# Mixture-of-experts tiles cut in four quarters of 32 rows instead of two halves of 64, with three quarters' weights copied, in a two-block transformer kernel

## The chip, the cores and the metric

One core of one Trainium2 chip runs the whole program. The metric is the device time of one execution in microseconds (us), lower is better. Three runs of the kernel before gave 2169.46, 2170.88 and 2175.67 us, so the median is 2170.88 us.

## The reference, cut to what matters

The program is a transformer block followed by two further blocks (`l` = 0 and 1). Each of these two ends in a mixture of experts over 768 tokens (block 0: 512 of the sequence and 256 of the context) or 512 tokens (block 1). A token has 1024 values; there are 16 experts in 4 groups; each token takes one group and in it two experts.

```python
a = jnp.einsum('nd,edf->nef', h, w_gate[g])      # 1024 -> 256, per expert
u = jnp.einsum('nd,edf->nef', h, w_up[g])        # 1024 -> 256
hid = jax.nn.silu(a) * u * combine[:, g, :, None]
out = out + jnp.einsum('nef,efd->nd', hid, w_down[g])   # 256 -> 1024
```

So block 0 has 1536 (token, expert) rows and block 1 has 1024. An expert's weights in float32 are 2 MB for gate and up together and 1 MB for down, 48 MB over the 16 experts of a block. Worked out from the reference and its inputs, the rows per expert are 72 to 132 in block 0 and 35 to 89 in block 1.

## The kernel before, in words

`Router` and `Dispatch` work out which expert each token takes and sort the rows into **tiles of 128 rows**. A tile has two **halves** of 64 rows, each half of one expert; `pairs_bound` gives 20 tiles in block 0 and 16 in block 1, whatever the routing. `mo.pace` spreads the experts over the tiles, and `k.last_pair[e]` holds the last tile that needs expert e.

`Experts` then runs over the tiles t. `tensor` (PE) does, per tile: gate/up, 8 chunks of 128 in the contraction, each chunk one matmul for the low half (L2356, moving operand straight from the expert's place) and one for the high half (L2357, moving operand from a copy `mo.wgu`); then down of tile t-1 (L2337, L2338, the high half from the copy `mo.wd`); then the transposes of `hid` (L2368) and of the gathered rows of tile t+2 (L2322). The two halves write partitions 0 to 63 and 64 to 127 of one PSUM bank. `gpsimd` (POOL) gathers a tile's 128 rows from DRAM by an indirect DMA (L2516), `mo.xg` has two buffers, so the gather of tile t waits for the transposes of tile t-2. ACT (ScalarE) and DVE (VectorE) copy the high half's weights (L2412, L2478 for gate/up; L2418, L2484 for down), bring transposes out of PSUM, and ACT stores the finished tile (L2402). All of these buffers are double.

The weights come through `ExpertLoads.fill` on the SP queue, in an order that is written out. There are three **places** of 3 MB; expert e goes to place e % 3:

```python
sp.wait_ge(self.gu_full[0], last + (self.gu_full[1] + 1))     # L2241
for j in range(2):
    sp.dma_start(k.places[:, a, j, :], self.w[e, j])...       # L2242, gate/up, 2 x 1 MB
if e:
    self.announce_down(sp, e - 1)                             # waits until down of e-1 landed
sp.wait_ge(k.gu_landed[a].sem, ...)                           # L2246
...
sp.dma_start(k.places[:, a, 2, :], self.w[e, 2])...           # L2249, down, 1 MB
```

Before an expert's gate/up goes out, SP waits until the last tile that used the place has done its gate/up; before its down, until that tile has done its down (`y_full`). An announcement lets the copying engines use what landed. While an expert's down is under way, the gate/up of the next may be issued.

After the last tile every stage meets (L3290), and `CombineProject` (block 0) or `Combine` (block 1) gathers each token's two result rows (L2618, L2539) and adds them to the residual rows `k.X`, six tiles of 1024 columns.

Of the kernel before, what the change touches and what calls it, by code (L numbers as in the profile page):

```python
# [17 lines left out]
F32 = mybir.dt.float32  # L18
# [33 lines left out]
PLACES = 3  # L52
HALF = 64
# [12 lines left out]
def shape_constants():  # L66
# [40 lines left out]
    halves = [2 * pairs_bound(n * P) for n in (NT, ST)]  # L107
    c["pace"] = np.tile(np.array([[(x + 1) * h // NEXP for x in range(NEXP)] for h in halves], np.float32), (P, 1, 1))
# [1853 lines left out]
class Router(Stage):  # L1962
# [4 lines left out]
    def __init__(self, k, l, tiles, rows):  # L1967
        super().__init__(k)
        self.l, self.tiles, self.rows_out = l, tiles, rows
# [6 lines left out]
        self.consts = k.small_landed.reserve(64 + 16 * (1 + (len(tiles) > ST)))  # L1976
        self.freed = k.places_free.reserve(1)

    def gpsimd(self, pool, ch):
        k = self.k  # L1980
        loads = [(k.mo.iota, k.C["iota"]), (k.mo.token, k.C["token"]), (k.mo.before, k.C["before"]),
                 (k.mo.pace, k.C["pace"][:, self.l, :])]
        loads += k.gate_loads(self.l, 5, 1 + (len(self.tiles) > ST))
        for dst, src in loads:
            pool.dma_start(dst, src).then_inc(k.small_landed.sem, 16)
        pool.wait_ge(k.small_landed.sem, self.consts + 16 * len(loads))
# [48 lines left out]
    def await_consts(self, eng):  # L2035
        eng.wait_ge(self.k.small_landed.sem, self.consts + 64 + 16 * (1 + (len(self.tiles) > ST)))
# [70 lines left out]
def pairs_bound(tokens):  # L2107

    return ((2 * tokens - NEXP) // HALF + NEXP + 1) // 2


class Dispatch(Stage):


    def __init__(self, k, n, router):
        super().__init__(k)
        self.n, self.m, self.router = n, pairs_bound(n * P), router
# [4 lines left out]
    def tensor(self, pe):  # L2122
# [8 lines left out]
        for u in range(2 * n):  # L2131
            last = pe.matmul(self.banks.bank(2)[:, 0:2 * self.m], mo.row_hot[:, u, :], mo.pair_hot[:, u, 0:2 * self.m],
# [3 lines left out]
    def vector(self, dve, ch):  # L2136
# [16 lines left out]
        at, at_pair, at_row = (x[:, 0:2 * n] for x in (mo.at, mo.at_pair, mo.at_row))  # L2153
# [14 lines left out]

        do(dve.tensor_scalar(mo.count, mo.count, 1.0 / HALF, None, ALU.mult))
        count_of(mo.halves, mo.count, NEXP, 2 * n - 1, ALU.is_gt)  # L2170
        do(dve.tensor_scalar(mo.halves, mo.halves, 1.0, None, ALU.add))
        do(dve.tensor_tensor_scan(mo.end, mo.ones[:, 0:NEXP], mo.halves, 0.0, ALU.mult, ALU.add))

        do(dve.tensor_scalar(mo.spare, mo.end[:, NEXP - 1:NEXP], -1.0, float(2 * m), ALU.mult, ALU.add))
# [4 lines left out]
        do(dve.tensor_tensor(mo.first, mo.end, mo.halves, ALU.subtract))  # L2179
        do(dve.scalar_tensor_tensor(rank, over_tokens(mo.first), float(HALF), rank, ALU.mult, ALU.add))  # L2180
        for i in range(2):
# [4 lines left out]
        count_of(at_pair, at_row, 2 * n, m - 1, ALU.is_ge)  # L2186
        do(dve.scalar_tensor_tensor(at_row, at_pair, -float(P), at, ALU.mult, ALU.add))
        pairs = mo.pair_hot[:, 0:2 * n, 0:m]
        ch.step(dve.tensor_tensor(pairs, mo.iota[:, 0:m].unsqueeze(1).to_broadcast((P, 2 * n, m)),
                                  at_pair.unsqueeze(2).to_broadcast((P, 2 * n, m)), ALU.is_equal))  # L2190
# [3 lines left out]
        for i in range(2):  # L2194
            half = pairs[:, n * i:n * i + n, :]
            dve.tensor_tensor(mo.pair_hot[:, n * i:n * i + n, m:2 * m], half,
# [4 lines left out]
        ended = mo.ended[:, 0:2 * m * NEXP].rearrange("p (h e) -> p h e", e=NEXP)  # L2201
        do(dve.tensor_tensor(ended, mo.iota[:, 0:2 * m].unsqueeze(2).to_broadcast((P, 2 * m, NEXP)),
                             mo.end.unsqueeze(1).to_broadcast((P, 2 * m, NEXP)), ALU.is_ge))
        do(dve.tensor_reduce(mo.expert[:, 0:2 * m], ended, AXX, ALU.add))
        do(dve.tensor_scalar(mo.expert[:, 0:2 * m], mo.expert[:, 0:2 * m], float(NEXP - 1), None, ALU.min))
        dve.tensor_copy(k.half_expert[:, 0:2 * m], mo.expert[:, 0:2 * m])
        do(dve.tensor_scalar(mo.last, mo.end, 0.5, -0.5, ALU.mult, ALU.add))
        count_of(mo.count, mo.last, NEXP, m - 1, ALU.is_ge)
        dve.tensor_copy(k.last_pair[:, :], mo.count)
# [6 lines left out]
class ExpertLoads:  # L2216


    def __init__(self, k, l, A, router, dispatch, gu_full, y_full):
        self.k, self.w, self.gu_full, self.y_full = k, A["experts"][l], gu_full, y_full  # L2220
        self.n0 = k.rg.lend(self)
        self.freed, self.lists = router.freed, dispatch.ready
# [3 lines left out]
        self.ready = k.experts_ready.reserve(2 * NEXP)  # L2226
        self.early = []

    def fill(self, sp):
        k = self.k  # L2230
        sp.wait_ge(k.weights_used, self.n0)
        for e in range(NEXP):
            a = e % PLACES
            if e == PLACES - 1:
                sp.wait_ge(k.places_free.sem, self.freed + 1)
            if e == PLACES:
                sp.wait_ge(k.lists_ready.sem, self.lists + 1)
            if e >= PLACES:
                last = sp.value_load(k.last_pair[0:1, e - PLACES:e - PLACES + 1], min_val=0, max_val=63)
                sp.wait_ge(self.gu_full[0], last + (self.gu_full[1] + 1))  # L2240
            for j in range(2):  # L2241
                sp.dma_start(k.places[:, a, j, :], self.w[e, j]).then_inc(k.gu_landed[a].sem, 16)  # L2242
            if e:
                self.announce_down(sp, e - 1)
# [10 lines left out]
        for n in self.early:  # L2255
            k.rg.load(sp, n)
# [1145 lines left out]
```

## Time and profile before

| | |
|---|---|
| runs, median (lowest to highest) | 2170.88 us (2169.46 to 2175.67) |
| the profiled execution, its own time | 2169.99 us |
| its span, first to last instruction | 2168.2 us |
| granted TensorE clock, mean | 0.976 of full |
| PE, DVE, ACT, POOL busy | 94%, 46%, 28%, 9% of the span |
| DMA | 311.64 MB, mean 144 GB/s |
| Experts stage of block 0, first gate/up to last down | 1374.6 to 1612.5 us |
| Experts stage of block 1, the same | 1949.0 to 2141.6 us |

Shares over the span are means of stages that are bound by different things; the two Experts stages are a fifth of the time. Times in the rows are microseconds from the start of the span, durations in microseconds unless ns stands there.

### The profile page before, as it was taken

The page shows a single profiled execution, that of the slowest core. Times are in us where ns is not written, and L with a number is a line of the kernel's source. Part 1 is how long each engine was busy: PE and PEld are TensorE (multiplying, and loading weights), DVE is VectorE, ACT ScalarE, POOL GpSimd, SP SyncE. Part 2 cuts the span into 40 slices and gives each one's busy share as a digit, 9 for nine tenths or more (in the row PEclk, how much of TensorE's full clock was granted, in tenths as well). Part 3 has the DMA queues.
Part 4 walks back from the last instruction along what each step waited for, and adds up shares of the span by engine and source line. Part 5 has one row for each costly group of instructions (what it writes and reads, how often), then busy time and mean ns, then how long its engine had stood idle before and what let it go on. Part 6 is the DMA issues. An engine that isn't in the chain of part 4 may idle for free.

```text
span 2168.2 us, 26578 instructions
## 1 busy us (share of the span) xinstructions
PE 2033.5 (94%) x10088; PEld 1107.5 (51%) x10088; DVE 989.7 (46%) x1778; ACT 616.2 (28%) x1302; POOL 188.7 (9%) x222
## 2 busy tenths in 40 slices
PE   7999999999999999898998998999989999989994
PEld 4555874444444444456456745533335688463331
DVE  2002771487777001378736524423218577253333
ACT  2002660100000001422225503334325566033331
POOL 3000110011111000022100000101001000011101
PEclk9999999999999999999999999999999999989997
DMA  8433101576765321211201004678853200067885
GB/s 266 133 78 127 40 11 39 193 242 227 244 241 211 117 68 60 84 39 40 73 6 60 18 3 168 248 296 309 299 183 135 76 3 2 1 253 286 336 327 207
DMA packets 103868, 311.64 MB, mean 144 GB/s; under 512 B 8839, under 2 KB 42791, under 8 KB 85312
## 3 DMA queue, kind: packets, MB, share of 16 engines
q1 hardware_dynamic: 73360, 178.50, 23.5%
q0 software_dynamic: 22576, 103.09, 13.7%
q10 hardware_dynamic: 7808, 28.35, 3.3%
q8 instruction: 84, 1.38, 0.3%
q14 instruction: 40, 0.33, 0.0%
HBM read 280.47 MB, written 34.68 MB: 145 GB/s over the span
## 4 chain that ended last, share of the span: by engine, by line
PE 76%; issue 7%; DVE 5%; DMA 5%; PEld 3%; ACT 2%; SPq 0%; POOL 0%; PEldq 0%; POOLq 0%; DVEq 0%; ACTq 0%
PE ps L2857 14%; PE ps L312 8%; PE ps L337 8%; PE ps L2356 7%; PE ps L1623 6%; PE ps L806 5%; DMA wide<-in_experts 4%; PE ps L852 4%; PE ps L827 4%; PE ps L2660 4%; PE ps L2337 3%; PE ps L1599 2%; PEld ps L1379 2%; PE ps L1028 1%; PE ps L1379 1%
## 5 line engine op out<-in xcount | busy, mean ns | idle before, releaser
L2857 PE MATMUL ps<-wide 128*128 128x512 f32 x704 | 306.0, 594 | 2.3 <-issue 1.3
L2356 PE MATMUL ps<-wide,Z 128*64 x576 | 254.9, 595 | 2.1 <-DVE Z L2459 2.1
L2357 PE MATMUL ps<-T,Z 128*64 128x512 f32 x576 | 254.9, 596 | 0.0
L2857 PEld LDWEIGHTS ps<-wide 128*128 128x128 f32 x704 | 132.6, 190 | 171.7 <-issue 170.4
L2356 PEld LDWEIGHTS ps<-wide,Z 128*64 128x64 f32 x576 | 75.9, 137 | 152.0 <-issue 152.0
L1623 PE MATMUL ps<-wide 128*128 128x512 f32 (+1 forms) x384 | 148.3, 543 | 0.5 <-issue 0.5
L2337 PE MATMUL ps<-wide,Z 128*64 x288 | 131.2, 599 | 4.9 <-ACT Z L2418 4.9
L1150 DVE SCALAR_TENSOR_TENSOR Z<-Z,wide 128x2048 f32<-128x2048 f32 x56 | 131.6, 2350 | 2.8
L2338 PE MATMUL ps<-Z 128*64 128x512 f32 x288 | 131.3, 599 | 0.0
L806 PE MATMUL ps<-T 64*128 64x256 f32 (+1 forms) x888 | 109.7, 377 | 7.8 <-DVE nm L940 5.9
L1379 PE MATMUL ps<-wide 128*128 128x512 f32 x256 | 114.6, 607 | 1.8 <-issue 1.1
L373 ACT ACTIVATE T<-ps 128x512 f32<-128x512 f32 (+2 forms) x139 | 70.6, 536 | 133.5 <-PE ps L1379 111.1
L1623 PEld LDWEIGHTS ps<-wide 128*128 128x128 f32 x384 | 71.8, 190 | 68.6 <-issue 65.3
L872 ACT ACTIVATE T<-T,nm 128x768 f32<-128x768 f32 (+3 forms) x112 | 86.7, 775 | 68.0 <-DVE nm L940 68.0
L312 PE MATMUL ps<-wide 128*128 128x512 f32 x224 | 98.6, 602 | 6.7 <-POOLq L3290 3.9
L806 PEld LDWEIGHTS ps<-T 64*128 64x128 f32 x888 | 86.1, 191 | 29.2 <-issue 14.0
L3176 DVE TENSOR_TENSOR X<-ps,X 128x512 f32<-128x512 f32 x16 | 11.1, 692 | 196.6 <-PE ps L312 103.7
L852 PE MATMUL ps<-T,Z 128*64 128x128 f32 x1504 | 98.9, 278 | 0.4 <-ACT wide L888 0.4
L337 PE MATMUL ps<-wide 128*128 128x512 f32 x224 | 97.1, 594 | 0.3
L375 DVE COPY T<-ps 128x512 f32<-128x512 f32 (+2 forms) x113 | 69.7, 637 | 59.8 <-PE ps L1379 49.8
L2873 ACT ACTIVATE Z<-ps 128x512 f32<-128x512 f32 x22 | 13.1, 597 | 293.2 <-PE ps L2857 293.1
L2412 ACT ACTIVATE T<-wide 128x2048 f32 x36 | 68.6, 1906 | 78.5 <-SPq L2246 52.6
(383 smaller groups left out, 3029.5 us busy)
## 6 DMA issues: line engine op xcount, KB each, us to landing
wide<-in_experts SPq DMA_DIRECT2D x96, 1024.0 KB, 7.9
Z<-in_mod_w POOLq DMA_DIRECT2D x32, 1024.0 KB, 5.2
moe_out<-Z ACTq DMA_DIRECT2D x36, 512.0 KB, 5.8
X<-in_mod_w POOLq DMA_DIRECT2D x16, 1024.0 KB, 5.3
wide<-in_w_gate SPq DMA_DIRECT2D x22, 512.0 KB, 5.3
wide<-in_w_up SPq DMA_DIRECT2D x22, 512.0 KB, 6.8
wide<-in_w_in SPq DMA_DIRECT2D x10, 1024.0 KB, 9.1
wide<-in_w_down SPq DMA_DIRECT2D x10, 1024.0 KB, 5.2
```

The costliest lines, as they stand in the source:

```text
L312: last = pe.matmul(self.banks.bank(u0 + i)[0:self.rows, 0:cn], self.lhs(k0 + c, t), w[:, c, :], start=(k0 + c == 0), stop=(k0 + c == self. ...
L337: last = pe.matmul(self.banks.bank(u0 + i)[:, 0:cn], self.lhs(k0 + c, t), w[:, c, :], start=(k0 + c == 0), stop=(k0 + c == self.nk - 1))
L806: last = pe.matmul(self.S(i, h)[:, at:at + m], q, keys, start=True, stop=True)
L852: last = pe.matmul(k.ps[64 * h:64 * h + 64, 7, t * P:(t + 1) * P], u["values"][b](h), self.PT[:, j % 2, h, b * P:(b + 1) * P], start=(b * ...
L1150: ins = dve.scalar_tensor_tensor(acc, w, by, acc, ALU.mult, ALU.add)
L1379: last = pe.matmul(self.banks.bank(u), w, k.HT[:, c, 0:SEQ], start=(c == 0), stop=(c == DK - 1))
L1623: last = pe.matmul(self.lin.bank(u)[:, 0:cn], k.HT[:, c, t * P:(t + 1) * P], w[:, c % 4, :], start=(c == 0), stop=(c == DK - 1))
L2337: pe.matmul(ps[low, 5 + hf, :], mo.hidT[:, p, c, low], w.columns(e, 2, at), start=(c == 0), stop=(c == 1))
L2338: last = pe.matmul(ps[high, 5 + hf, :], mo.hidT[:, p, c, high], mo.wd[:, p, at:at + 512], start=(c == 0), stop=(c == 1))
L2356: pe.matmul(ps[low, p, :], mo.xT[:, p, c, low], w.columns(e, j, at), start=(c == 0), stop=(c == DK - 1))
L2357: last = pe.matmul(ps[high, p, :], mo.xT[:, p, c, high], mo.wgu[:, p, j, at:at + 512], start=(c == 0), stop=(c == DK - 1))
L2857: last = pe.matmul(self.gu.bank(u)[:, 0:self.n], w, self.rhs(c), start=(c == 0), stop=(c == DK - 1))
```

## The change

A tile of 128 rows now has four **quarters** of 32 rows (`QUARTER = 32`), each of one expert. `quads_bound` gives 16 tiles in block 0 and 12 in block 1. Worked out from the routing, in block 0 tile t is expert t in all four quarters, except that one quarter of tile 13 is expert 12; in block 1 the tiles are 0 0 0 1, 1 1 2 2, 2 3 3 3, 4 4 4 5, 5 5 6 6, 6 7 7 7, 8 8 8 9, 9 9 10 10, 10 11 11 11, 12 12 12 13, 13 13 14 14, 14 15 15 15. Each quarter's matmul writes 32 partitions. Quarter 0 reads the place, quarters 1, 2, 3 read copies: DVE copies for quarters 1 and 2, ACT for quarter 3. There is one buffer where there were two for the copies, `xg`, `xT`, `ysb`, `silu`, `hid`; the gate/up copies are made in two parts (chunks 0 to 3 after `gu_half`, chunks 4 to 7 after `gu_full`).

There are four gate/up places (in `wide`) and four down places (in `T`). The down of expert e is loaded after the gate/up of expert e + `LAG`. To make room, residual tiles 3 to 5 (block 0) or 2 and 3 (block 1) are written to DRAM by POOL in the Router stage and read back by SP after the last tile is stored; `ysb`, `xT`, `xg` and the row gate of block 1 lie in `k.X`. The gates of block 0 are loaded at the end by SP instead of by POOL in the Router.

```diff
-PLACES = 3
-HALF = 64
+PLACES = 4
+QUARTER = 32
+LAG = 3
-def pairs_bound(tokens):
-    return ((2 * tokens - NEXP) // HALF + NEXP + 1) // 2
+def quads_bound(tokens):
+    return ((2 * tokens - NEXP) // QUARTER + NEXP + 3) // 4
@@ Router.gpsimd
-        loads += k.gate_loads(self.l, 5, 1 + (len(self.tiles) > ST))
-        for dst, src in loads:
+        for dst, src in loads + [self.spill]:
             pool.dma_start(dst, src).then_inc(k.small_landed.sem, 16)
@@ ExpertLoads.fill
-        for e in range(NEXP):
-            a = e % PLACES
+        for e in range(PLACES):
             if e == PLACES - 1:
                 sp.wait_ge(k.places_free.sem, self.freed + 1)
...
+            self.load_gate_up(sp, e)
+        self.router.await_rows(sp)
+        for e in range(PLACES):
+            self.load_down(sp, e)
+        for e in range(PLACES):
+            self.announce_gate_up(sp, e)
+        for e in range(PLACES):
+            self.announce_down(sp, e)
+        sp.wait_ge(k.lists_ready.sem, self.lists + 1)
+        for e in range(PLACES, NEXP + LAG):
+            if e - PLACES >= PLACES:
+                self.announce_down(sp, e - PLACES)
+            if e < NEXP:
+                sp.wait_ge(self.gu_full[0], self.last_of(sp, e - PLACES) + (self.gu_full[1] + 1))
+                self.load_gate_up(sp, e)
+                self.announce_gate_up(sp, e)
+            d = e - LAG
+            if d >= PLACES:
+                sp.wait_ge(self.y_full[0], self.last_of(sp, d - PLACES) + (self.y_full[1] + 1))
+                self.load_down(sp, d)
         self.announce_down(sp, NEXP - 1)
...
+        sp.wait_ge(self.y_full[0], self.y_full[1] + self.m)
+        for dst, src in self.gates:
+            sp.dma_start(dst, src).then_inc(k.gates_landed.sem, 16)
+        sp.wait_ge(self.y_stored[0], self.y_stored[1] + 16 * self.m)
+        for dst, src in self.back:
+            sp.dma_start(dst, src).then_inc(k.tiles_back.sem, 16)
+    def announce_gate_up(self, sp, e):
+        k, a = self.k, e % PLACES
+        sp.wait_ge(k.gu_landed[a].sem, self.gu_landed[a] + 32 * (e // PLACES + 1))
+        sp.drain().then_inc(k.gu_ready.sem, 1)
@@ Experts.tensor
+        def gate_up(t, e, j):
+            for c in range(4 * j, 4 * j + 4):
+                at = 512 * (c % 4)
+                for q, rows in enumerate(quarters):
+                    w_rows = mo.wgu[:, q - 1, j, at:at + 512] if q else w.gate_up(e, j, at, 512)
+                    last = pe.matmul(ps[rows, t % 2, :], mo.xT[:, c, rows], w_rows, start=(c == 0), stop=(c == DK - 1))
+            return last
@@ Experts.vector, the new order
+        first_rows(0)
+        x_out(0)
+        last_rows(0)
+        for t in range(m):
+            if t + 1 < m:
+                first_rows(t + 1)
+                x_out(t + 1)
             self.after(dve, self.silu_ready, t + 1)
...
+            if t + 1 < m:
+                last_rows(t + 1)
+            if t:
+                y_out(t - 1)
             down_copy(t)
+        y_out(m - 1)
@@ Experts.gpsimd
         for t in range(self.m):
-            gather(t)
+            if t:
+                self.after(pool, self.x_transposed, t)
```

The SP queue in the steady part of block 0, before (L2242 is an expert's gate/up, L2249 its down, the TENSOR_LOAD reads the last tile that used the place):

```order
L2242 DMA wide<-in_experts 128x2048 [waits moe_gu_full]
L2242 DMA wide<-in_experts 128x2048
L2249 DMA wide<-in_experts 128x2048 [waits down_landed_0,gate_up_landed_1,moe_y_full]
L2239 TENSOR_LOAD last_pair
L2239 ISA x2
L2240 REGISTER_ALU
L2242 DMA wide<-in_experts 128x2048 [waits moe_gu_full]
L2242 DMA wide<-in_experts 128x2048
L2249 DMA wide<-in_experts 128x2048 [waits down_landed_1,gate_up_landed_2,moe_y_full]
```

And in the changed kernel, from the down of expert 4 on (L2280 is gate/up, L2284 down):

```order
L2284 DMA T<-in_experts 128x2048 [waits moe_y_full]
L2275 TENSOR_LOAD last_quad [waits down_landed_0]
L2275 ISA x2
L2253 REGISTER_ALU
L2280 DMA wide<-in_experts 128x2048 [waits moe_gu_full]
L2280 DMA wide<-in_experts 128x2048
L2275 TENSOR_LOAD last_quad [waits gate_up_landed_0]
L2275 ISA x2
L2258 REGISTER_ALU
L2284 DMA T<-in_experts 128x2048 [waits moe_y_full]
```

The wait for an expert's down to land stood behind the next gate/up's issue; now it stands ahead of it, and a second TENSOR_LOAD stands between gate/up and down.

The POOL queue, block 0, before (gathers of the tiles' rows):

```order
L2516 DMA Z<-moe_rows,row_token 128x1024 [waits small_landed,rows_stored,stage_done]
L2516 DMA Z<-moe_rows,row_token 128x1024
L2516 DMA Z<-moe_rows,row_token 128x1024 [waits moe_x_transposed] x18
```

And changed:

```order
L2554 DMA X<-moe_rows,row_token 128x1024 [waits small_landed,rows_stored,stage_done]
L2554 DMA X<-moe_rows,row_token 128x1024 [waits moe_x_transposed] x15
```

The second gather went out at once; now each but the first waits for the transposes of the tile just before it.

## Rows read from the trace of the kernel before

**Rows 1.** The page, part 1: engine, busy us, share of the span, instructions.

```profile
PE 2033.5 (94%) x10088; PEld 1107.5 (51%) x10088; DVE 989.7 (46%) x1778; ACT 616.2 (28%) x1302; POOL 188.7 (9%) x222
```

**Rows 2.** Timeline, PE, one tile of block 0: start, us, engine, line, operation, tiles, count.

```profile
1441.78 0.44 PE L2368 MATMUL ps<-ident,Z 128*128 128x128 f32 x2
1442.05 1.04 PE L2322 MATMUL ps<-ident,Z 128*128 128x128 f32 x8
1443.02 0.64 PE L2356 MATMUL ps<-wide,Z 128*64 x1
1443.02 0.64 PE L2357 MATMUL ps<-T,Z 128*64 128x512 f32 x1
...
1454.71 0.64 PE L2356 MATMUL ps<-wide,Z 128*64 x1
```

**Rows 3.** Groups by line, whole span: count, then busy us and mean ns.

```profile
L2356 PE MATMUL ps<-wide,Z 128*64 x576 | 254.9, 595 | 2.1 <-DVE Z L2459 2.1
L2478 DVE COPY T<-wide 128x2048 f32 x36 | 44.4, 1233 | 62.0 <-SPq L2246 58.4 <-issue 3.5
L2412 ACT ACTIVATE T<-wide 128x2048 f32 x36 | 68.6, 1906 | 78.5 <-SPq L2246 52.6 <-issue 13.9 <-DVEq L3290 12.0
L2484 DVE COPY Z<-wide 128x1024 f32 x36 | 24.6, 684 | 0.0
```

**Rows 4.** Timeline, PE: first gate/up of block 0, then of block 1, last down.

```profile
1374.60 0.64 PE L2356 MATMUL ps<-wide,Z 128*64 x1 [1.05 <-DVE Z L2459]
...
1611.94 0.59 PE L2337 MATMUL ps<-wide,Z 128*64 x1
...
1949.02 0.64 PE L2356 MATMUL ps<-wide,Z 128*64 x1 [1.04 <-DVE Z L2459]
...
2141.04 0.59 PE L2337 MATMUL ps<-wide,Z 128*64 x1
```

**Rows 5.** Chain of waits, block 1: start, us, what; the first and another of eight.

```profile
1970.88 11.56 DMA wide<-in_experts
1983.90 11.31 DMA wide<-in_experts
```

**Rows 6.** Stages of both blocks: busy us of the engines, then PEclk, DMA share, GB/s.

```profile
1374.00:1613.00 239.00, 235.33 (x1152) 88.19 (x1152) 71.24 (x99) 93.96 (x120) 20.52 (x18) 0.99 0.72 266
1949.00:2142.00 193.00, 187.18 (x920) 70.12 (x920) 64.38 (x78) 66.06 (x79) 15.25 (x14) 1.00 0.78 292
```

**Rows 7.** Timeline, SP queue, block 1: issues of gate/up (x2) and down (x1).

```profile
1903.41 0.81 SPq L2242 DMA_DIRECT2D wide<-in_experts  x2
1910.85 0.33 SPq L2249 DMA_DIRECT2D wide<-in_experts  x1
...
1982.54 0.33 SPq L2249 DMA_DIRECT2D wide<-in_experts  x1
1983.52 1.62 SPq L2242 DMA_DIRECT2D wide<-in_experts  x2
...
1996.55 0.89 SPq L2242 DMA_DIRECT2D wide<-in_experts  x2
```

**Rows 8.** Expert weights, the down issued at 1910.85, Router stage of block 1.

```profile
DMA to landing us min/median/max: 4.8/4.8/4.8
```

**Rows 9.** Expert weights, the gate/up issued at 1520.32, block 0.

```profile
DMA to landing us min/median/max: 5.5/7.2/8.8
```

**Rows 10.** Expert weights, the down issued at 1515.28, block 0.

```profile
DMA to landing us min/median/max: 6.4/6.4/6.4
```

**Rows 11.** Gathers of tile rows, block 0, 1380 to 1610.

```profile
DMA to landing us min/median/max: 5.0/7.8/11.5
```

**Rows 12.** Timeline, PE, mod stage: four column quarters, 16 passes of 512 columns.

```profile
465.53 1.92 PE L1127 MATMUL ps<-Z,wide 128*32 128x512 f32 x16
```

**Rows 13.** Timeline, PE: passes after a pause, end of block 0 and of block 1.

```profile
1607.27 1.11 PE L2337 MATMUL ps<-wide,Z 128*64 x1 [2.19 <-ACT Z L2418]
...
1608.17 1.06 PE L2337 MATMUL ps<-wide,Z 128*64 x1
...
1610.65 0.59 PE L2337 MATMUL ps<-wide,Z 128*64 x1
...
2137.99 0.64 PE L2337 MATMUL ps<-wide,Z 128*64 x1 [2.67 <-ACT Z L2418]
...
2138.47 0.59 PE L2337 MATMUL ps<-wide,Z 128*64 x1
```

**Rows 14.** Timeline, start of block 0: the second tile's gate/up (PE).

```profile
1384.54 0.64 PE L2356 MATMUL ps<-wide,Z 128*64 x1
```

More of the change, by code:

```diff
@@ L2304, in after @@
         eng.wait_ge(s[0], s[1] + tiles)
-    def run(self, eng, prologue, step, epilogue):
-        prologue()
-        for t in range(self.m):
-            step(t // 2, t % 2, t == self.m - 1)
-        epilogue(self.m // 2, self.m % 2)
     def tensor(self, pe):
@@ L2335, in down @@
                 for c in range(2):
-                    at = 1024 * c + 512 * hf
-                    pe.matmul(ps[low, 5 + hf, :], mo.hidT[:, p, c, low], w.columns(e, 2, at), start=(c == 0), stop=(c == 1))
-                    last = pe.matmul(ps[high, 5 + hf, :], mo.hidT[:, p, c, high], mo.wd[:, p, at:at + 512],
-                                     start=(c == 0), stop=(c == 1))
+                    for q, rows in enumerate(quarters):
+                        at = 512 * hf
+                        w_rows = mo.wd[q - 1][c][:, at:at + 512] if q else w.down(e, 1024 * c + at, 512)
+                        last = pe.matmul(ps[rows, 5 + hf, :], mo.hidT[:, c, rows], w_rows, start=(c == 0), stop=(c == 1))
             last.then_inc(self.y_full[0], 1)
-        keep_awake(pe, k, 7, 17 if m > 16 else 30)
+        keep_awake(pe, k, 7, 17 if m > ST * 3 else 30)
         x_transposes(0)
-        e = w.expert_of(pe, 0)
-        before = None
+        e, before = w.expert_of(pe, 0), None
         for t in range(m):
-            p = t % 2
-            self.after(pe, self.gu_act, t + 1)
-            self.after(pe, self.gu_dve, t + 1)
+            self.after(pe, self.first_act, t + 1)
+            self.after(pe, self.first_dve, t + 1)
             self.after(pe, self.x_out_act, t + 1)
@@ L2353, in tensor @@
                 self.after(pe, self.hid_ready, t - 1)
-            for c in range(DK):
-                j, at = c // 4, 512 * (c % 4)
-                pe.matmul(ps[low, p, :], mo.xT[:, p, c, low], w.columns(e, j, at), start=(c == 0), stop=(c == DK - 1))
-                last = pe.matmul(ps[high, p, :], mo.xT[:, p, c, high], mo.wgu[:, p, j, at:at + 512],
-                                 start=(c == 0), stop=(c == DK - 1))
-            last.then_inc(self.gu_full[0], 1)
-            after = w.expert_of(pe, 2 * t + 2) if t + 1 < m else None
+            gate_up(t, e, 0).then_inc(self.gu_half[0], 1)
+            self.after(pe, self.last_act, t + 1)
+            self.after(pe, self.last_dve, t + 1)
+            gate_up(t, e, 1).then_inc(self.gu_full[0], 1)
+            after = w.expert_of(pe, 4 * t + 4) if t + 1 < m else None
             if t:
@@ L2500, in step @@
                                      ALU.mult, ALU.mult).then_inc(self.hid_ready[0], 1)
-            if peeled and t == 0:
-                x_out(0, 1)
-            else:
-                y_out(b - (p == 0), 1 - p)
-            if t + 2 < self.m:
-                x_out(b + 1, p)
+            if t + 1 < m:
+                last_rows(t + 1)
+            if t:
+                y_out(t - 1)
             down_copy(t)
-        self.run(dve, first, step, lambda b, p: y_out(b - (p == 0), 1 - p))
+        y_out(m - 1)
@@ L3004, in two_blocks @@
         mo.either, mo.rank, mo.prior, mo.tmp = (zb(NT * NEXP, "p (n e) -> p n e", n=NT) for _ in range(4))
-        mo.count, mo.halves, mo.end, mo.first, mo.last, mo.pace, mo.late = (zb(NEXP) for _ in range(7))
+        mo.count, mo.quarters, mo.end, mo.first, mo.last, mo.pace, mo.late = (zb(NEXP) for _ in range(7))
         mo.spare = zb(1)
-        mo.at, mo.at_pair, mo.at_row = (zb(2 * NT) for _ in range(3))
+        mo.at, mo.at_quad, mo.at_row = (zb(2 * NT) for _ in range(3))
         mo.weight = sb("weight", [P, 2, NT])
@@ new lines, in two_blocks @@
+        mo.both = [k.Z[:, at[0] + 2 * D * i:at[0] + 2 * D * (i + 1)].rearrange("p (s n) -> p s n", s=2) for i in range(ST)]
+        mo.ended = zb(4 * bound * NEXP)
+        mo.expert = zb(4 * bound)
+        mo.row_hot = zb(2 * NT * P, "p (u n) -> p u n", u=2 * NT)
+        mo.quad_hot = zb(4 * NT * bound, "p (u n) -> p u n", u=2 * NT)
+        k.down_places = T[:, 0:PLACES * SLOT].rearrange("p (a n) -> p a n", a=PLACES)
+        mo.wgu = k.Z[:, 0:6 * SLOT].rearrange("p (q j n) -> p q j n", q=3, j=2)
```

406 lines of the change are left out of this document (205 added, 201 removed).

## The prediction

> **What bounds the kernel now.** I read the page first, then the chain of waits, then the timelines of PE and of the SP queue in the two Experts stages, which alone change much. PE is busy 94% of the span, the other engines under half [rows 1]. In block 0's Experts stage PE is busy for 235.3 of 239 us [rows 6]: it bounds. A tile starts 11.69 us after the one before (1443.02 to 1454.71), and low and high half start at the same moment, so one pass of both costs one pass [rows 2]. By line that pass is 254.9 us / 576 = 0.44 us, 0.4275 without gaps [rows 3]. The tile is 16 such passes for gate/up (6.84 us), 8 for down (3.42) and 1.43 of transposes. In block 1 PE is busy 187.2 of 193 us, but the chain runs through eight loads of expert weights of some 11.5 us each [rows 5, 6]; gate/up loads go out 13.03 us apart there (1983.52 to 1996.55) [rows 7], more than a tile. So block 1 is already bound by its weight loads over most of its length, PE close behind. From the first gate/up to the end of the last down block 0 takes 1612.53 - 1374.60 = 237.9 us and block 1 2141.63 - 1949.02 = 192.6 [rows 4], 430.5 together. Those are the numbers to beat.
>
> **PE's part.** 36 tiles become 28. A pass of four quarters should cost what a pass of two halves costs: elsewhere in this kernel 16 passes of 32 columns take 1.92 us, four rounds at 0.43 and a tail [rows 12]. So the tile stays 11.69 us, and PE's work falls by 8 x 11.69 = 94 us. This counts only where PE is what is waited for.
> The Trainium skill, "TensorE: Matmul & The Clock Gate", section "Measured speedup vs the span model", has four tiles of 32 rows at 3.07 times one, which speaks against the change: gate/up and down would take 10.26 x 4 / 3.07 = 13.4 us, the tile 14.8. The trace's sixteen passes disagree with it, and 14.8 is still less than the load period below, so the sum would grow only in the tails, by some 12 us.
>
> **Copies.** Per tile DVE makes 4 copies at 1.23 us for gate/up and 2.6 us for down (1.23 and twice 0.68), ACT three at 1.91 [rows 3]: 7.6 and 5.7 us, with the drains of PSUM about 10 and 8. Both fit in 11.69 us, and each has 8.3 us between the event that frees its buffer and the matmul that needs it. I cost them at nothing except where the down copy follows a late landing (2.6 us), and behind the last tile, where PE has nothing else: y_out and the copy, 3.3 us in block 0 and 3.8 in block 1.
>
> **The loads, which decide.** Each expert now costs the SP queue a strict row: gate/up out, wait until landed, read a register, down out, wait until landed, read a register. Nothing overlaps, where before the next gate/up was out 0.98 us behind the down (1982.54 to 1983.52; of it 0.65 us is the read) [rows 7]. With nothing else moving, gate/up lands after 7.44 us (1903.41 to 1910.85) and a down after 4.8 [rows 7, 8]. The period P per expert is then 7.44 + 0.65 + 4.8 + 0.65 = 13.5 us: the lower bound. In the stage a gather and a store of 0.5 MB each go beside it. There, with no other weight in flight, a gate/up took 8.8 us from its second issue, 9.3 from its first, and a down 6.4 [rows 9, 10]: 9.3 + 6.4 + 1.3 = 17.0, the upper bound, since those rows have a gather and a store each 11.69 us. I take P0 = 16 in block 0, where each expert's tile brings one gather and one store, and P1 = 15.5 in block 1, with three quarters as many.
> By the Trainium skill, "DMA: Bandwidth & Descriptors", section "Anatomy of one DMA", a transfer costs 2.0 us and its bytes at 436 GB/s: 6.8 and 4.4 us here. The rows have 7.44 and 4.8; by the page the sum would be some 16 us lower.
>
> **The start of a stage.** With one `xg`, the gather of tile 2 waits for the transposes of tile 1, which PE does at 7.9 us after its start T. A gather takes 7.8 us [rows 11], and PE takes those transposes before gate/up of tile 1, which so starts at T + 17 instead of T + 9.9 [rows 4, 14]. From there tiles follow at 11.69: gate/up of tiles 1, 2, 3 end at T + 23.9, 35.6, 47.3. In later tiles the gather has 10.8 us and is mostly hidden.
>
> **Block 0.** Gate/up of expert 7 goes out at T + 48 (it needs tile 3), lands at 56.9, so down of expert 4 goes out at 57.6 and down of expert 12 at 57.6 + 8 P0. It lands 6 later and is copied (2.6). PE then still has four downs, two sets of transposes, two gate/ups and the last copy: 13.7 + 2.9 + 13.7 + 3.3 = 33.6. Sum: 99.8 + 8 P0 = 227.8 us with P0 = 16, against 237.9: **-10**.
>
> **Block 1.** 16 experts in 12 tiles. Gate/up 6 goes out at T + 35.6 (tile 2), gate/up 7 at 45.2, down 4 at 54.8, down 12 at 54.8 + 8 P1. Tile 9 needs experts 12 and 13: down 13 lands 11.2 later, copy 2.6, then three downs (10.3), transposes 1.4, one gate/up 6.8, last copy 3.8: 22.3. Sum: 90.9 + 8 P1 = 214.9 with P1 = 15.5, against 192.6: **+22**.
>
> **The rest.** (a) Clock: after a pause of 2.2 us PE's passes started 0.87 us apart, so at the half of the two levels, for four passes, and that cost 1.7 us; after one of 2.67 us in block 1 the next pass came 0.48 us later, at full clock [rows 13]. Three pauses more lie on the path: +3, bounds 0 and +5. (b) Four downs (4 MB) now go out just ahead of gather 0, in both blocks: +4, bounds 0 and two times the 4 MB alone. (c) Dispatch compares and reduces over longer lists: +1. (d) Its constants now wait for a spill of 1.5 or 1 MB: +1, bounds 0 and a landing of 8. (e) Reading the residual tiles back competes with the gathers of the results: +2; their own landing is hidden behind the first tiles' additions, the gates behind the last store. Together +11, from 0 to +26.
> Sum: -10 + 22 + 11 = **+23 us**. The profiled execution's own time is 2169.99, its span 1.8 less, and the median 0.9 above it, so I forecast **2193 us**.
> In general the change is 8 (P0 + P1) - 239.8 + 11: 16 us for each us of the period. It is nought at a mean P of 14.3.
>
> **Rivals.**
> *B: gathers and stores slip into the queue's gaps.* Around each landing the weight queue moves nothing; if the 0.5 MB transfers fall there, P is 13.5 and the change -13, 2157 us. It decides from a mean P under 14.3. For it: the row of gate/up alone. Against: the gather's and the store's moments hang on down and transposes, just when the next down is under way, as in the rows with 6.4 and 8.8 [rows 9, 10]. Within 0.3% (6.5 us, about what a measurement of this kernel can tell from no change) it is P from 13.9 to 14.7, faster below. 0.23: faster 0.14, same 0.09.
> *A: the loads keep up.* Four places let weights run ahead, PE bounds: block 0 198, block 1 152 us, 81 less, with the rest about 2097. It needs loads that overlap, and the order rows show none. 0.04.
> *C: half clock.* If the clock falls at every wait for a down and stays for the tile, PE's 10.3 us double, block 0 becomes 23.4 us a tile: +90 there and some 20 in block 1, 2300. The row shows four passes, not twenty-four [rows 13]. 0.03.
> *D: the quarters run two by two*, or the change doesn't do side by side what it says: the tile takes 21.9 us, 16 x 21.9 = 351 and 12 x 21.9 = 263 us, together 183 more, 2360. Against it [rows 12]. 0.02.
>
> **How the numbers follow.** My forecast has 0.68, its own range P from 14.7 to 17: 2177 to 2217 us. With P = 13.5 at the low end (2157), and the unknown costs up to +26 at the high end with P = 17 (2230), both a little trimmed as they would have to coincide, and a few us for gathers that slip into the gaps wholly, the range is 2152 to 2226. Left out are A, C, D and some tails, 0.2 at most. Faster: 0.14 of B and 0.04 of A, 0.18. Same: 0.09 and 0.02 of my own low edge, 0.11. Slower: 0.71.
>
> **What would show it.** In the SP timeline of the changed kernel down and gate/up issues must alternate with no overlap, 15 to 17 us for a pair. The chain of waits in both Experts stages must run through expert loads, PE idle 3 to 5 us a tile in block 0, more in block 1. Block 0 should last about 228 us, block 1 about 215. PE's passes must start 0.43 us apart for four quarters, and gate/up of tile 1 about 17 us after tile 0. A PE without gaps, or pairs of loads under 14 us apart, would prove me wrong.

## The result and the profile after

The changed kernel took 2214.16 us (median of 4 runs, 2212.63 to 2216.36), the kernel before 2172.04 (4 runs, 2169.46 to 2175.67) beside it. The ratio is 1.0181, 95% interval 1.0158 to 1.0204: slower by 1.8%. The forecast was 2193, range 2152 to 2226.

The page of the changed kernel, part 1 (as [rows 1]):

```profile
span 2211.7 us, 28534 instructions
PE 1975.8 (89%) x10968; PEld 1071.7 (48%) x10968; DVE 1101.1 (50%) x1878; ACT 651.2 (29%) x1286; POOL 178.2 (8%) x214
```

PE is busy for 57.7 us less and the span is 43.5 us longer: PE waits more, as forecast. The two Experts stages, in the view of windows (as [rows 6]: busy us of PE, PEld, DVE, ACT, POOL, then PEclk, DMA share, GB/s):

```profile
1383.00:1621.00 238.00, 201.40 (x1688) 66.19 (x1688) 135.42 (x157) 114.37 (x111) 15.53 (x15) 0.93 0.66 239
1966.00:2184.00 218.00, 155.06 (x1264) 50.15 (x1264) 106.85 (x117) 79.60 (x71) 12.27 (x11) 0.86 0.62 227
```

Fewer bytes move than before, and they move more slowly: 239 GB/s over 238 us is 57 MB in block 0 where it was 266 GB/s over 239 us, 64 MB, and 227 over 218 us is 49 MB in block 1 where it was 292 over 193 us, 56 MB. The 7 MB are, as an estimate from the sizes, one expert more that is loaded ahead of the stage (3 MB) and four tiles fewer that gather and store (4 MB). From first gate/up to last down, block 0 takes 1383.16 to 1620.77 = 237.6 us (237.9 before), block 1 1966.23 to 2183.87 = 217.6 (192.6 before). Of the 43.5 us, 25.0 lie in block 1's stage and nothing in block 0's; 6.3 lie between block 0's Router and its first gate/up, 5.6 between block 0's last tile and block 1's Router (most of it in the combine), 3.4 from there to block 1's first gate/up, and 1.2 behind the last tile; 2.2 came before block 0's Router, where nothing was changed.

The SP queue in block 0's steady part (as [rows 7]; L2280 is gate/up, L2284 down):

```profile
1466.96 0.81 SPq L2280 DMA_DIRECT2D wide<-in_experts  x2
1476.05 0.33 SPq L2284 DMA_DIRECT2D T<-in_experts  x1
1484.08 0.80 SPq L2280 DMA_DIRECT2D wide<-in_experts  x2
...
1577.14 18.33 SPq L2284 DMA_DIRECT2D T<-in_experts  x4
```

And the chain of waits there (start, us, what; compare [rows 5]):

```profile
1467.33 8.02 DMA wide<-in_experts
1475.37 0.06 issue
1475.43 0.27 SPq L2275
1475.73 0.15 SPq L2275
1475.87 0.05 issue
1476.05 7.33 DMA T<-in_experts
...
1484.45 8.26 DMA wide<-in_experts
```

That is the strict row: gate/up, land, read a register, down, land, read. The down of expert 4 goes out at 1441.27 and that of expert 12 at 1577.14, so a pair takes 16.98 us. In block 1 it is 2022.98 to 2146.02, 15.38 a pair. A pair is 3 MB.

By line and form (as [rows 3]: count, busy us, mean ns, idle before and its releaser):

```profile
L2369 PE MATMUL ps<-wide,X 128*32 x448 | 201.4, 603 | 2.1 <-DVE X L2518 2.1
L2385 PE MATMUL ps<-T,gw 128*32 128x512 f32 (+1 forms) x560 | 122.6, 700 | 84.5 <-ACT T L2442 84.5
L2442 ACT ACTIVATE T<-T 128x2048 f32 x28 | 53.5, 1912 | 159.3 <-SPq L2294 150.7 <-DVE X L2525 4.2 <-issue 2.4
L2496 DVE COPY Z<-wide 128x2048 f32 x28 | 34.3, 1223 | 37.1 <-PE ps L2369 33.6 <-issue 3.6
```

PE's 84.5 us of waiting stand against ACT's copy of the down (L2442); in block 0 they are 29.0 us in 9 waits, 3.2 us each. That copy in turn waited 150.7 us for the announcement on SP (L2294). A gate/up pass of four quarters costs 603 ns to its end, one of two halves 595: four stand side by side. The mean of the down's passes, 700 ns where it was 599 before (L2337), shows the lower clock after the waits (below).

### The profile page after: what moved, and what is told of

It is laid out like the page before. It is cut to its first block, busy times and chain, and to the rows that moved or that the text cites. A ratio compares the mean times of both kernels' runs of the same rounds, so it can differ in the third digit from the quotient of the medians.

```text
span 2211.7 us, 28534 instructions
## 1 busy us (share of the span) xinstructions
PE 1975.8 (89%) x10968; PEld 1071.7 (48%) x10968; DVE 1101.1 (50%) x1878; ACT 651.2 (29%) x1286; POOL 178.2 (8%) x214
## 4 chain that ended last, share of the span: by engine, by line
PE 74%; DMA 12%; DVE 5%; issue 5%; ACT 2%; SPq 1%; POOL 1%; DVEq 0%; POOLq 0%; ACTq 0%
PE ps L2900 14%; PE ps L313 8%; PE ps L338 8%; PE ps L1624 6%; PE ps L1380 5%; DMA wide<-in_experts 5%; PE ps L807 5%; PE ps L853 4%; PE ps L2369 4%; PE ps L828 4%; DMA T<-in_experts 4%; PE ps L2699 4%; PE ps L2385 2%; PE ps L1382 2%; PE ps L1600 2%
## 5 line engine op out<-in xcount | busy, mean ns | idle before, releaser
L2900 PE MATMUL ps<-wide 128*128 128x512 f32 x704 | 307.7, 596 | 2.3 <-issue 1.3
L2369 PE MATMUL ps<-wide,X 128*32 x448 | 201.4, 603 | 2.1 <-DVE X L2518 2.1
L2369 PE MATMUL ps<-Z,X 128*32 128x512 f32 x1344 | 201.8, 603 | 0.0
L2385 PE MATMUL ps<-T,gw 128*32 128x512 f32 (+1 forms) x560 | 122.6, 700 | 84.5 <-ACT T L2442 84.5
L2385 PE MATMUL ps<-wide,gw 128*32 128x512 f32 x224 | 122.2, 697 | 0.0
L1380 PE MATMUL ps<-wide 128*128 128x512 f32 x256 | 113.6, 602 | 1.9 <-issue 1.0
L2385 PEld LDWEIGHTS ps<-T,gw 128*32 128x32 f32 x560 | 30.9, 126 | 172.0 <-issue 172.0
L2369 PEld LDWEIGHTS ps<-wide,X 128*32 128x32 f32 x448 | 47.6, 111 | 128.2 <-issue 128.2
L313 PE MATMUL ps<-wide 128*128 128x512 f32 x224 | 100.3, 610 | 6.7 <-POOLq L3341 3.9
L2442 ACT ACTIVATE T<-T 128x2048 f32 x28 | 53.5, 1912 | 159.3 <-SPq L2294 150.7
```

Of the source, the lines that this page charges most:

```text
L313: last = pe.matmul(self.banks.bank(u0 + i)[0:self.rows, 0:cn], self.lhs(k0 + c, t), w[:, c, :], start=(k0 + c == 0), stop=(k0 + c == self. ...
L1380: last = pe.matmul(self.banks.bank(u), w, k.HT[:, c, 0:SEQ], start=(c == 0), stop=(c == DK - 1))
L2369: last = pe.matmul(ps[rows, t % 2, :], mo.xT[:, c, rows], w_rows, start=(c == 0), stop=(c == DK - 1))
L2385: last = pe.matmul(ps[rows, 5 + hf, :], mo.hidT[:, c, rows], w_rows, start=(c == 0), stop=(c == 1))
L2900: last = pe.matmul(self.gu.bank(u)[:, 0:self.n], w, self.rhs(c), start=(c == 0), stop=(c == DK - 1))
```

## Experiments

Two theories of the 43.5 us stood at the start. **T1**: the loads' strict row (wait for a landing before the next issue) sets the stages. **T2**: it is the copies, three quarters of every weight through DVE and ACT. A third is about `LAG`: a down stands behind three gate/ups that are not needed yet. All ratios below are against the kernel before, run beside the experiment. T is the start of a stage's first gate/up, and a **pair** is one expert's gate/up and down on the SP queue.

### The announcement moved behind the next issue (e1_behind, e3_both)

The loop of the loads; `LAG` stays 3 in e1_behind and is 1 in e3_both:

```diff
         for e in range(PLACES, NEXP + LAG):
-            if e - PLACES >= PLACES:
-                self.announce_down(sp, e - PLACES)
             if e < NEXP:
                 sp.wait_ge(self.gu_full[0], ...)
                 self.load_gate_up(sp, e)
+            if e - LAG - 1 >= PLACES:
+                self.announce_down(sp, e - LAG - 1)
+            if e < NEXP:
                 self.announce_gate_up(sp, e)
```

> The changed kernel with one edit: the wait for an expert's down to land stands behind the issue of the next gate/up, as in the kernel before; LAG stays 3. Theory S (the strict row of loads on the SP queue sets the stage): the period of a gate/up and a down falls from 17.0 and 15.4 us to about 13 (the 13.03 of the kernel before), block 0 by some 20 us to about 217, block 1 by some 17 to about 200, the whole to about 2176. Rival R (the 16 DMA engines move what they can, so order does not matter): periods and time stay, 2214 within 5. Rival C (single-buffered copies on DVE and ACT hold the tiles): no change either.

Measured: 2186.39 us, ratio 1.0051 (1.0032 to 1.0069). Block 0 takes 213.9 us, block 1 210.6; a pair takes 13.9 us in block 0 (downs of experts 4 and 12 at 1441.37 and 1552.57) and 14.2 in block 1 (2002.11 and 2115.40). One edit in the order of waits took two thirds of the loss away, and no byte less was moved, which rules out rival R. Not all of it came as expected: the pairs stayed 1 us above the 13 us, block 1 took 210.6 us instead of 200, and the time is 10 us above 2176. The next experiment shows why.

> As e1_behind, and LAG 1 in place of 3, so that the down of expert e goes out behind the gate/up of e+1. S: beside the overlap the queue also fills the early holes, in which it waits for tiles to finish; block 0 about 197 us (PE then bounds at 11.69 a tile), block 1 about 195, the whole about 2150, below the kernel before's 2172. R: at most 5 us gained, since the bytes are the same. C: no change, 2214.

Measured: 2148.46 us, ratio 0.9868 (0.9829 to 0.9906): faster than both kernels. Block 0 203.0 us (197 expected), block 1 188.8 (195 expected). From e1_behind to e3_both only the lag differs. What it did is seen in the SP timeline of e1_behind, block 1:

```profile
2024.96 0.33 SPq L2285 DMA_DIRECT2D T<-in_experts  x1
2035.22 0.80 SPq L2281 DMA_DIRECT2D wide<-in_experts  x2
2043.23 0.33 SPq L2285 DMA_DIRECT2D T<-in_experts  x1
```

The gate/up at 2035.22 waits 10 us for its place (three experts ahead, it needs a tile that PE has not reached), and the downs that PE needs are queued behind it. With lag 1 the first of these downs goes out at T + 35.6 in block 0 instead of T + 59.2.

### The lag alone (e2_lag1)

As e3_both, with the announcement left ahead of the issue:

```diff
-LAG = 3
+LAG = 1
...
-            if e - PLACES >= PLACES:
-                self.announce_down(sp, e - PLACES)
+            if e - LAG - 1 >= PLACES:
+                self.announce_down(sp, e - LAG - 1)
```

> The changed kernel with the down of expert e loaded behind the gate/up of expert e+1 instead of e+3, and still every load waited for before the next is issued. With the wait behind the next issue as well, the shorter lag brought 38 us (2186.4 to 2148.5). Theory: the strict row of loads sets the period, so in whatever order they go a pair still takes 16.5 to 17 us in block 0 and 15 to 15.5 in block 1; only the two ends of the stage move: stages of 228 to 236 us and 213 to 219 us, time 2200 to 2215. Rival: the lag alone is at fault (a down that is needed early stands behind three gate/ups that are not), overlap or none: then most of the 38 us come here too, 2175 to 2185, stages of 220 and 200.

Measured: 2213.29 us, ratio 1.0176 (1.0139 to 1.0213), the same as the changed kernel. So the lag alone brings nothing and the lag behind overlapped loads 1.8%: the strict row binds first. The pair in block 0 is 17.2 us (1419.62 to 1591.36, ten pairs). The expectation failed in one place: block 0 was 229.1 us, but block 1 223.7 instead of 213 to 219, its pair at 16.4. Why shows when three queues of e2_lag1 are read together (timelines of SP, POOL and ACT's queue, block 1):

```profile
2036.72 1.45 POOL L2554 DMA_INDIRECT X<-moe_rows,row_token  x1 [14.84 <-PE ps L2361]
2037.69 0.80 SPq L2280 DMA_DIRECT2D wide<-in_experts  x2
2038.52 0.33 ACTq L2461 DMA_DIRECT2D moe_out<-X  x1
2050.15 0.33 SPq L2284 DMA_DIRECT2D T<-in_experts  x1
2055.60 0.81 SPq L2280 DMA_DIRECT2D wide<-in_experts  x2
2063.54 0.33 SPq L2284 DMA_DIRECT2D T<-in_experts  x1
```

And its chain:

```profile
2038.07 11.39 DMA wide<-in_experts
2050.15 4.75 DMA T<-in_experts
2055.98 6.85 DMA wide<-in_experts
2063.54 4.72 DMA T<-in_experts
```

Gather, gate/up and store go out within 1.8 us of each other, and the gate/up takes 11.39 us; the next one, with no tile beside it, takes 6.85. A pair without a tile beside it is 13.4 us (2050.15 to 2063.54), one with a tile 17.9 (2037.69 to 2055.60). The tile runs when the loads release it, so its transfers always meet a load.

### Tiny copies (e4_tiny)

```diff
-            dve.tensor_copy(mo.wgu[:, 0, 0, :], w.gate_up(experts[t][0], 0, 0, SLOT))
+            dve.tensor_copy(mo.wgu[:, 0, 0, 0:cols(t)], w.gate_up(experts[t][0], 0, 0, cols(t)))
...
+def cols(t):
+    return 64 if t else SLOT
```

and the same for every other copy of weights. From tile 1 on the three quarters so compute with the first tile's weights.

> The changed kernel in which, from the second tile on, the copies of the three quarters' weights move 64 columns in place of 2048 or 1024 (those quarters compute with the first tile's weights, so this leaves out the copying). S: the loads still bound; only the copies behind a late landing (2.6 us) and behind the last tile (3 us) go, 5 to 6 us a block, 2203. C: the stages fall to what PE needs, 198 and 152 us, 2110. R: as S.

Measured: 2211.35 us, ratio 1.0168 (1.0127 to 1.021); block 0 235.1, block 1 216.6. All the copying from tile 1 on is worth 2.5 us in block 0 and 1.0 in block 1, less than the 5 to 6 a block that were expected (2203), so T2 falls.

### Small loads (e5_small)

The row of waits stays; the kernel leaves out three quarters of the bytes from expert 4 on:

```diff
-            sp.dma_start(k.gu_places[:, a, j, :], self.w[e, j]).then_inc(k.gu_landed[a].sem, 16)
+            sp.dma_start(k.gu_places[:, a, j, 0:512 if e >= PLACES else SLOT], self.w[e, j][:, 0:512 if e >= PLACES else SLOT]).then_inc(k.gu_landed[a].sem, 16)
```

and the same for the downs.

> The changed kernel with the loads of experts 4 to 15 cut to a quarter of their columns (512 of 2048; the rest keeps the weights of an earlier expert, so this leaves out three quarters of the bytes). S and R: weights are in time, PE bounds, block 0 about 198 us, block 1 about 155, the whole 2112. A quarter-size pair still has to cost the two fixed waits, so pairs under 9 us. C: copies still bind, block 0 stays above 225, the whole above 2190. It also gives the tile's own pitch: 11.7 us if four quarters run side by side and the copies fit.

Measured: 2119.13 us, ratio 0.9744 (0.9687 to 0.9802); block 0 200.0, block 1 166.2, tiles 11.68 us apart in block 0. So in block 0, without the loads' time, the four quarters bring what PE's sum says (198). In block 1 they don't: 166.2 us where 155 was expected. There the order of the row still costs time with small loads: the gate/up at 2006.22 goes out only when PE's gate/up has ended (1999.16 plus 7.05 us) and freed its place, and the down behind it waits too. A smaller load shortens a strict row as well, so this run alone does not tell bytes from order; e1_behind and e3_both do, with all the bytes.

### What is in the pair: gathers and stores (e6_gather, e10_alone)

```diff
+            if t >= 4:
+                pool.dma_start(k.mo.xg[:, 0:16], self.rows[0:P, 0:16]).then_inc(self.x_landed[0], 16)
+                continue
             pool.indirect_dma_start(k.mo.xg, None, self.rows,
```

From tile 4 on the gathered rows are left out.

> The changed kernel, but from tile 4 on the gather of a tile's 128 rows is replaced by a load of 16 columns of fixed rows (8 KB); it leaves out most of the gathered data, so it computes less. The order, the waits and the stores stay. Theory: a part of the period of a pair of loads is contention with the 0.5 MB gathers and stores: without the gathers the period falls from 17.0 to about 15.5 us in block 0 and from 15.4 to 14.5 in block 1, with 10 to 14 us off block 0 and 5 to 9 off block 1, time 2190 to 2200. Rival: the gathers fall into the gaps, or the period is latency and waits alone: it stays at 16.5 to 17 and 15 to 15.4, time 2208 to 2214.

Measured: 2196.73 us, ratio 1.0102 (1.0055 to 1.0149); block 0 227.6, block 1 212.0; the pair 15.7 us in block 0 (1443.72 to 1569.38) and 14.8 in block 1 (2014.44 to 2132.60). The gathers are 1.3 us of the pair in block 0, 0.6 in block 1.

e10_alone leaves out the stores from tile 4 on as well, and makes the first four larger:

```diff
-            act.dma_start(self.y[t], mo.ysb).then_inc(self.y_stored[0], 16)
+            if t >= 4:
+                act.dma_start(self.y[t][:, 0:16], mo.ysb[:, 0:16]).then_inc(self.y_stored[0], 16)
+                return
+            act.dma_start(self.y[t:m:4].rearrange("a p d -> p a d"), ...).then_inc(self.y_stored[0], 16)
```

> The changed kernel with the gathers from tile 4 on cut to 8 KB, as in the run with small gathers, and the stores from tile 4 on cut to 8 KB too (each of the first four stores writes four or three tiles instead, before the steady part); it leaves out most gathered and stored data. From expert 8 on nothing but expert weights moves. Theory: what is above the bound of 13.5 us in the period is contention with the gathers and stores, so the period falls from 15.7 and 14.8 us (small gathers) to 13.3 to 13.9 in both blocks; time 2175 to 2185. Rival: the rest is waiting of another kind (the tile that must free the place, the two engines' copies): the period stays at 14.5 or above; time 2190 to 2197.

Measured: 2191.92 us, ratio 1.0077 (1.0052 to 1.0102). Block 0 takes 222.8 us, block 1 211.7. The time and the mean pair, 14.9 us in block 0 and 14.5 in block 1, missed the expectation and lie where the rival had them. Gathers and stores together are so 2.1 us of the pair in block 0 and 0.9 in block 1, not all of what is above the bound. The pairs from expert 8 on, where nothing else moves, take 14.0 in both blocks (downs of experts 8 and 12 at 1510.24 and 1566.16, and at 2069.72 and 2125.60), just above it. The chain of e10_alone at the end of that stretch:

```profile
1538.98 5.11 DMA T<-in_experts
...
1545.16 6.97 DMA wide<-in_experts
...
1552.82 4.75 DMA T<-in_experts
...
1558.64 6.81 DMA wide<-in_experts
...
1566.16 4.82 DMA T<-in_experts
```

Here a pair is 13.3 us (1552.82 to 1566.16): near the bound of 13.5 that was put together from the Router's rows [rows 7, 8]. What the averages have above it are single gate/ups of 8 to 9 us (one of 11.74 at 1454.25, early in block 0, where the large stores are), and a gate/up at 1516.07 that went out only when PE had freed its place, which is the rival's kind of wait. For a gate/up of 9.31 in block 1 (2045.80) no cause was found.

### The start of a stage (e9_xg2)

A second `xg` buffer, in a residual tile more that is spilled; gather t waits for the transposes of tile t - 2.

```diff
-            if t:
-                self.after(pool, self.x_transposed, t)
+            if t >= 2:
+                self.after(pool, self.x_transposed, t - 1)
```

> The changed kernel with a second buffer for the gathered rows alone: gathers run two tiles ahead, one more residual tile is spilled and read back; loads stay in their strict row with lag 3. Theory: gate/up of tile 1 starts at T + 10 to T + 12 instead of T + 19, and since the strict row of loads starts with tile 3's gate/up, the whole row moves 7 to 9 us forward in block 0 and 6 to 8 in block 1; the periods stay at 17.0 and 15.4; time 2196 to 2205. Rival: the first places' loads are already late, so that the stall hides under them and only its end shows: 0 to 3 us, 2210 to 2216.

Measured: 2200.16 us, ratio 1.0109 (1.0065 to 1.0153); gate/up of tile 1 at T + 10.5 in both blocks, first single down at T + 49.3 instead of T + 58.1 in block 0, at T + 48.6 instead of T + 56.7 in block 1; stages 225.2 and 209.9. The row of loads moved forward, by 8.8 and 8.1 us: the stall is in the time even though loads bind, because the loads wait for the first tiles' places. Block 0 gained more than that, as its pair fell to 16.3 us (1435.67 to 1566.31) instead of staying at 17.0; why is open. Of the 20 us gained in the two stages 8 were lost outside them, and the time fell by 14.

### The spill (e7_spill)

```diff
-        for dst, src in loads + [self.spill]:
+        for dst, src in loads:
...
-        for dst, src in self.rows_gate:
+        for dst, src in [self.spill] + self.rows_gate:
```

and the constants' waits are 64 instead of 80.

> The changed kernel with the spill of the residual tiles issued behind the landing of the router's constants, which no longer wait for it; it does the same work. In the changed kernel's chain the spill before block 1's Dispatch takes 11.85 us. Theory: that wait is on the path, and Dispatch starts 3 to 8 us earlier over the two blocks; the Experts stages stay at 236 to 238 and 216 to 218 us; time 2204 to 2211. Rival: the expert downs or the lists end last right behind it, so that taking it away moves nothing: 2212 to 2216.

Measured: 2216.32 us, ratio 1.0195 (1.0161 to 1.023): nothing gained, as the rival had it. The changed kernel's chain ahead of block 1's Dispatch, and e7_spill's in the same place:

```profile
1929.17 11.85 DMA rows_away<-X
```

```profile
1929.36 7.27 DMA Z<-const_pace
...
1936.92 0.71 POOL rows_away L1988
1937.63 15.77 DMA X<-mod_rows
```

The row gate, which stood behind the constants, now lands beside the spill and the gate/ups and takes 15.77 us, and the first gather waits for it. The wait moved, it did not go.

### The pieces together (e8_all, e12_early)

e8_all is e3_both with the second `xg` buffer and the spill moved; e12_early is the same without the spill's move.

> The overlapped loads with lag 1 (2148.5 us before), with the spill behind the constants as in the run beside it, and with a second buffer for the gathered rows, so that gathers run two tiles ahead (one more residual tile is spilled and read back for it). Theory: in both stages PE or a load pair near 12.5 us binds, and gate/up of tile 1 starts at T + 10 instead of T + 19: 7 to 9 us less in block 0, up to 7 in block 1, and 3 to 8 from the spill; stages of 194 to 197 and 180 to 186 us, time 2125 to 2138. Rival: in block 1 the loads bind from the first tile on, the start stall is only a shift there, and a gather two tiles ahead runs into the loads: 0 to 3 us from block 1, and longer loads; time 2138 to 2146.

> The overlapped loads with lag 1 and the second buffer for gathered rows, with the spill where the changed kernel has it (ahead of the constants' wait). It differs from the fastest run so far (2128.8 us) in the spill alone. Theory: as in the run with the spill moved alone, its place brings nothing, since what follows it in POOL's queue is late instead: 2125 to 2133, stages of 195 and 176 us. Rival: the spill's move was worth something once the loads overlap: 2134 to 2142.

Measured: 2128.83 us, ratio 0.9784 (0.9755 to 0.9813), and 2132.01, ratio 0.9809 (0.9769 to 0.9848); the intervals overlap, so the spill's place can't be told from nothing here either. Stages 195.0 and 175.8, and 194.6 and 172.4, block 1 shorter than the 180 to 186 expected. In e12_early the two stages read:

```profile
1385.00:1580.00 195.00, 190.37 (x1688) 65.06 (x1688) 137.71 (x157) 116.19 (x111) 16.98 (x14) 0.98 0.78 289
1928.00:2101.00 173.00, 147.10 (x1264) 50.51 (x1264) 107.01 (x118) 80.30 (x72) 16.40 (x10) 0.92 0.77 283
```

PE is busy for 190 of 195 us in block 0: there the change now meets its own bound. In block 1 it is 147 of 173 us, so something else still holds part of that stage. In e8_all's chain of block 0, whose long pieces are all PE's, gate/ups follow each other at 11.68 us:

```profile
1480.09 7.00 PE ps L2371 x64
1491.77 7.00 PE ps L2371 x64
1503.45 7.00 PE ps L2371 x64
```

## Why the prediction was right, and where its sizes were off

The sign and the mechanism held; some 20 of the 42 us were missing. With the measured pairs, 16.98 and 15.38, the prediction's formula 8 (P0 + P1) - 239.8 + 11 gives +30, so 7 us of what was missing are the size of P and some 12 lie in terms outside it: the ends of both stages and what surrounds them.

- **PE's part: right.** Four quarters cost what two halves cost, tiles 11.68 us apart where PE binds. The 3.07 times of the Trainium skill ("TensorE: Matmul & The Clock Gate", section "Measured speedup vs the span model") stands there for four row tiles, matmuls over 32 rows of the contraction (K = 32). The quarters here contract over all 128 and take 32 columns each (128*32 in the rows), so the figure was not for this shape; the estimate of 14.8 us a tile made from it did not come true, the tile took 11.68.
- **The loads decide: right, shown** by e3_both against e2_lag1. Gate/up and down alternate and the chain runs through them; the bytes are the same in both runs and the copies are ruled out by e4_tiny. That the wait for a landing moved ahead of the next issue is read in the order of the SP queue alone; this one place costs 28 us with lag 3 (2214 to 2186) and 65 with lag 1 (2213 to 2148).
- **P0: mis-sized.** The prediction put it at 16 between 13.5 and 17.0; it was 16.98, the upper bound. The step that failed is the choice inside the range, for which no working was given: 16 supposes that some loads run with no gather or store beside them, but once loads bind, each pair of block 0 brings a tile and the tile starts when the pair lets it, so they meet each time (the rows of e2_lag1; e6_gather and e10_alone price it at 2.1 us a pair). That the sum met the upper bound so closely is in part luck: from its issue to the next a gate/up took 9.3 us on average where the bound has 9.95, a down 7.7 where it has 7.05. The lower bound was right for what it says: 13.3 with nothing beside it. The Trainium skill, "DMA: Bandwidth & Descriptors", section "Anatomy of one DMA — SWDGE (gpsimd) path", fits 2.0 us and bytes at 436 GB/s to transfers that gpsimd issues. These loads are issued by SP, so 6.8 and 4.4 us are only an estimate from that page; e10_alone's last rows are some 0.5 above it, 7.2 to 7.4 for a gate/up from its first issue (6.81 to 6.97 from its second) and 4.75 to 5.11 for a down. With 16.98 the formula gives 235.6, measured 237.6.
- **P1: 15.5, measured 15.38.** Three tiles for four experts leave some pairs at 13.4 and others at 16 to 17. The formula gives 213.9, the stage took 217.6; +22 was +25.0. So here the period was right and the 3.7 us lie at the ends: down 4 went out at T + 56.7 instead of T + 54.8, and from down 12 to the end it took 37.9 us instead of 36.1.
- **The start: right in kind, 2 us short.** Gate/up of tile 1 came at T + 19.2 in block 0. The rows below show why: PE comes out of the wait for gather 0 at half clock. In block 1 it was T + 17.6.
- **Copies at nothing: right** (2.5 and 1.0 us, e4_tiny).
- **The rest: +11, measured +16.5** without the 2.2 ahead of the Router. Gather 0 in block 0 takes 9.2 us from its issue instead of 6.3 (1366.24 to the transposes at 1372.52), +3 where +4 was put (the landing itself took 4.5 us before, and PE's filler passes, L1028, hid it); the lists 1.3. The spill was put at +1 in all and has 11.85 us of block 1's chain, but all of the way from block 1's Router to its first gate/up grew by only 3.4, and what follows the spill would have been nearly as late (e7_spill). The way from block 0's last tile to block 1's Router was put at +2 and took 5.6 more. Of these 3.0 come before the next projection: a gather of results beside the read-back takes 9.82 us and is on the chain, where before 16.24 us of filler passes were. Another 1.5 are that projection's first 16 passes, 8.62 us (1649.69) instead of 7.11 (1638.48). The other 1.1 were not followed up. The +3 for the clock belongs into the stages; taken there, the rest was +8 against +16.5.

Behind block 0's last tile, in the changed kernel's chain:

```profile
1613.57 1.92 ACT T L2442
1615.62 5.15 PE ps L2385 x32
1620.80 0.70 DVE X L2527
1621.57 6.28 DMA moe_out<-X
...
1629.40 9.82 DMA Z<-moe_out,token_rows
```

So +23 came to +43.5 in the span: 10 us too little in block 0, 3 in block 1, 5.5 in the rest and 2.2 from a part that was not changed. Rival B (P at 13.5, because gathers and stores slip into the gaps) falls with the pairs of 16.98 and 15.38, and the rows of e2_lag1 show the opposite of slipping; A, C and D by the stages' times. One sum of the prediction is off: with P = 17 in both blocks its formula gives 2213 to 2214, not the 2217 of its own range.

## What to carry to other kernels

Fewer passes help only if the loads can use the time: before an engine's work is cut, write down the order of issues and waits on the load queue, and if a landing is waited for ahead of the next issue, add every landing in full. Here issuing the next load first, with a lag of one, and a second gather buffer turned 1.8% slower into 1.9% faster (e12_early). And where a tile is released by a load, its own transfers run into the next load, so take the price of a load beside them, not an average.

## What was unexpected

PE's clock after short waits. The timeline of the changed kernel at block 0's start:

```profile
1380.14 1.97 PE L2361 MATMUL ps<-ident,X 128*128 128x128 f32 x8 [2.78 <-DMA X<-moe_rows,row_token]
1383.16 1.06 PE L2369 MATMUL ps<-wide,X 128*32 x1 [1.05 <-DVE X L2518]
1384.01 1.06 PE L2369 MATMUL ps<-wide,X 128*32 x1
...
1386.54 0.59 PE L2369 MATMUL ps<-wide,X 128*32 x1
1386.97 0.59 PE L2369 MATMUL ps<-wide,X 128*32 x1
```

After a wait of 2.78 us the eight transposes take 1.97 us instead of 1.04 [rows 2] and the first passes are 0.85 us apart, at 1.2 GHz, then 0.43. The tiles that wait for their down show it too; here, in block 1, 32 matmuls take 5.55 us instead of 3.43:

```profile
2037.76 4.79 DMA T<-in_experts
...
2042.74 1.92 ACT T L2442
...
2044.79 5.55 PE ps L2385 x32
```

The granted clock of block 1's stage is 0.86 in the changed kernel where it was 1.00, and 0.92 in e12_early. With the same passes PE is busy for 201.4 and 155.1 us in the two stages, and for 190.4 and 147.1 in e12_early: the lower clock is some 11 and 8 us of PE's time; how much of it is on the path was not measured. The length of the wait alone does not tell it: ahead of block 1's last down PE waited 3.52 us (to 2180.23) and its passes still started 0.43 us apart. Some 2 us a wait is little beside the loads, but it lies behind a late landing, when everything else waits too.
